# Turning x to token order in the scan: 32x32 blocks on VectorE in place of 128x128 transposes on TensorE

## The reference, cut to what matters

```
xbc = silu(causal_dwconv(xbc, ...));  xs, bm, cm = split(xbc)
x  = xh * dt[..., None]                                      # by token and head
cb = einsum('bclgn,bcsgn->bcgls', cc, bc)                    # B times C, per group and chunk of 128
y_diag = einsum('bcgls,bgrcls,bcsgrp->bclgrp', cb, decay, x) # contracts over tokens s
y = y_diag + y_off + d_skip * xh                             # then gated, normed per group, projected
```

## Time and profile before

| | |
|---|---|
| Median of 3 runs | 1935.86 us |
| The profiled execution's own time | 1935.83 us |
| Its span in the profile | 1934.1 us |
| TensorE matmul busy | 1918.0 us, 99% |
| TensorE weight load busy | 1630.2 us, 84% |
| VectorE busy | 1264.0 us, 65% |
| ScalarE busy | 1083.7 us, 56% |
| GpSimd busy | 34.4 us, 2% |
| HBM read | 358.38 MB, 186 GB/s over the span |
| Transposes of x (L1587) | 64 instructions |

### The profile page before, as it was taken

One profiled execution on the slowest core, in us unless ns is written; L12 is line 12 of the kernel. 1 busy time (PEld: TensorE's weight loads), 2 busy tenths in 40 slices (PEclk: granted clock), 3 DMA queues, 4 the chain that ended last, 5 costly groups with the idle time before them and its releaser, 6 DMA issues.

```text
span 1934.1 us, 28955 instructions
## 1 busy us (share of the span) xinstructions
PE 1918.0 (99%) x10258; PEld 1630.2 (84%) x10258; DVE 1264.0 (65%) x1534; ACT 1083.7 (56%) x1474; POOL 34.4 (2%) x79
## 2 busy tenths in 40 slices
PE   9999999999999999999999999999999999999998
PEld 7888888888887878888888888888888888888886
DVE  6777788777868974544444555766766767745444
ACT  6567766677657764444344444666666666534443
POOL 1000000000000100000000000000000000000000
PEclk9999999999999999999999999999999999999999
DMA  7666666656655437666666565666666666665554
GB/s 244 189 192 177 196 190 192 191 171 196 200 153 138 132 127 213 194 192 194 193 193 195 175 229 191 201 184 186 194 191 190 187 186 191 188 200 193 192 193 141
DMA packets 294839, 361.53 MB, mean 187 GB/s; under 512 B 13104, under 2 KB 217968, under 8 KB 293360
## 3 DMA queue, kind: packets, MB, share of 16 engines
q1 hardware_dynamic: 294768, 360.59, 60.8%
HBM read 358.38 MB, written 2.16 MB: 186 GB/s over the span
## 4 chain that ended last, share of the span: by engine, by line
PE 98%; DVE 1%; ACT 1%; issue 0%; DMA 0%; DVEq 0%; SPq 0%; POOLq 0%; POOL 0%; ACTq 0%
PE ps L1405 35%; PE ps L1407 18%; PE ps L1390 14%; PE ps L1392 13%; PE ps L1391 13%; PE ps L1598 1%; PE ps L1526 1%; PE ps L1539 1%; PE ps L1550 0%; PE ps L1599 0%; PE ps L1587 0%; PE ps L1442 0%; DMA raw<-w_in 0%; ACT hi L449 0%; PE ps L1477 0%
## 5 line engine op out<-in xcount | busy, mean ns | idle before, releaser
L870 DVE TENSOR_TENSOR lo<-raw,hi 128x1024 fp32r<-128x1024 f32 x656 | 799.6, 1224 | 525.5 <-ACT hi L449 518.5
L1405 PE MATMUL ps<-uHL,hi 128*128 128x512 f32 x2944 | 1034.8, 396 | 0.3 <-ACT sgs L666 0.3
L449 ACT ACTIVATE hi<-raw 128x1024 fp32r<-128x1024 f32 x656 | 686.8, 1055 | 514.1 <-PE ps L1392 382.5
L1407 PE MATMUL ps<-uHL,lo 128*128 128x256 f32 x2944 | 823.7, 280 | 0.0
L1405 PEld LDWEIGHTS ps<-uHL,hi 128*128 128x128 f32 x2944 | 551.7, 187 | 130.6 <-issue 5.0
L1407 PEld LDWEIGHTS ps<-uHL,lo 128*128 128x128 f32 x2944 | 555.9, 189 | 0.0
L1392 PE MATMUL ps<-hi,aL 128*128 128x512 f32 x384 | 149.5, 389 | 0.0
L1392 PE MATMUL ps<-hi,hL 128*128 128x512 f32 x352 | 136.9, 389 | 0.0
L1391 PE MATMUL ps<-lo,hH 128*128 128x512 f32 x352 | 136.9, 389 | 0.0
L1390 PE MATMUL ps<-hi,hH 128*128 128x512 f32 x352 | 136.9, 389 | 0.0
L454 ACT ACTIVATE hb<-ps 128x512 f32<-128x512 f32 x92 | 54.7, 595 | 121.5 <-PE ps L1407 121.5
(11 more groups left out here) (195 smaller groups left out, 1654.7 us busy)
## 6 DMA issues: line engine op xcount, KB each, us to landing
raw<-w_in SPq DMA_DIRECT2D x265, 512.0 KB, 4.2
raw<-w_ffn_in SPq DMA_DIRECT2D x176, 512.0 KB, 3.8
raw<-w_ffn_out SPq DMA_DIRECT2D x88, 512.0 KB, 4.4
raw<-w_ssm_out SPq DMA_DIRECT2D x64, 512.0 KB, 4.4
raw<-w_attn_out SPq DMA_DIRECT2D x32, 512.0 KB, 4.3
raw<-w_o SPq DMA_DIRECT2D x32, 512.0 KB, 4.3
rows_b<-cum_rows SPq DMA_DIRECT2D x8, 1024.0 KB, 6.7
x_tok<-x SPq DMA_DIRECT2D x8, 256.0 KB, 6.5
```

Of the source, the lines that this page charges most:

```text
L449: act.activation(hi[:, s % SLOTS, :], raw[:, s % SLOTS, :], ACT.Copy).then_inc(hi_ready, 1)
L870: ve.tensor_tensor(lo[:, s % SLOTS, :], raw[:, s % SLOTS, :], hi[:, s % SLOTS, :].bitcast(F32), ALU.subtract).then_inc(lo_ready, 1)
L1405: pe.matmul(ps[:, pair + c, :], w_hi, uHL[:, kk].rearrange("p a n -> p (a n)"), start=kk == 0, stop=False)
L1407: last = pe.matmul(ps[:, pair + c, 0:SEQ], w_lo, uHL[:, kk, 0, :], start=False, stop=kk == k - 1)
```

## The change

TensorE keeps the two products of B and C and no longer transposes x; `turn_x` becomes `b_dot_c` and the semaphore `x_turned` becomes `bc_done`. VectorE gets a new step `x_turn(k, q)` behind each of the units u = 3, 4, 5, 6. Step q reads the 32 partitions q of x and issues four transposes, one for each 32-partition group j that it writes; each instruction turns eight blocks of 32x32 (4 channel tiles x 2 chunks), 256 numbers for each of its 32 partitions. They write `xd` directly; `ssd_inputs` then multiplies `xd` in place by `dt` instead of reading PSUM, and moves from behind u = 5 to behind u = 6, after the last `x_turn`. Everything else stays in its place.

```diff
+            def x_turn(k, q):
+                ve.wait_ge(sv_ready, k + 1)
+                src = sv[q * B32:(q + 1) * B32, 0:4, :].rearrange("p i (c n) -> p i c n", c=TT)
+                for j in range(P // B32):
+                    dst = xd[j * B32:(j + 1) * B32, :, :].rearrange("p c (i n) -> p i c n", i=4)
+                    ve.transpose(dst[:, :, :, q * B32:(q + 1) * B32], src[:, :, :, j * B32:(j + 1) * B32])
...
             def ssd_inputs(k):
-                ve.wait_ge(x_turned, k + 1)
+                ve.wait_ge(bc_done, k + 1)
                 ve.tensor_tensor(cbm[:].rearrange("p a n -> p (a n)"), ps[:, M, 0:3 * P],
                                  masks[:].rearrange("p a n -> p (a n)"), ALU.mult)
                 for c in range(TT):
-                    ve.tensor_tensor(heads(xd[:, c, :]), heads(ps[:, M + 1 + c, :]), bc(dtt[:, 0, c, ds(k * HG, HG)]),
+                    ve.tensor_tensor(heads(xd[:, c, :]), heads(xd[:, c, :]), bc(dtt[:, 0, c, ds(k * HG, HG)]),
                                      ALU.mult)
...
-            STEPS = dict(inputs=5, low=8, high=9, skip=12, gate=13, sum=17, mean=19)
+            STEPS = dict(inputs=6, low=8, high=9, skip=12, gate=13, sum=17, mean=19)
             def ssd_side(k, u, at=STEPS, older=True):
...
+                if 3 <= u < 7:
+                    x_turn(k, u - 3)
                 if u == at["inputs"]:
                     ve.drain()
                     ssd_inputs(k)
...
-            LAST_STEPS = dict(inputs=5, low=7, high=8, skip=11, gate=12, sum=13, mean=15)
+            LAST_STEPS = dict(inputs=6, low=7, high=8, skip=11, gate=12, sum=13, mean=15)
...
-            def turn_x(k, first=False):
+            def b_dot_c(k, first=False):
                 pe.wait_ge(sv_ready, k + 1)
                 if not first:
                     pe.wait_ge(y_skipped, k)
                 pe.matmul(ps[:, M, 0:2 * P], sv[:, 4, 0:P], sv[:, 5, :], start=True, stop=True)
-                pe.matmul(ps[:, M, 2 * P:3 * P], sv[:, 4, P:SEQ], sv[:, 5, P:SEQ], start=True, stop=True)
-                for c in range(TT):
-                    for i in range(4):
-                        last = pe.transpose(ps[:, M + 1 + c, i * P:(i + 1) * P], sv[:, i, c * P:(c + 1) * P], ident[:])
-                last.then_inc(x_turned, 1)
+                pe.matmul(ps[:, M, 2 * P:3 * P], sv[:, 4, P:SEQ], sv[:, 5, P:SEQ], start=True, stop=True) \
+                    .then_inc(bc_done, 1)
```

More of the change, by code:

```diff
@@ L61 @@
 W5 = 512
+B32 = 32
 U_KV = 0
@@ L238, in build @@
         conv_first, conv_done, sz_ready = sem("conv_first"), sem("conv_done"), sem("sz_ready")
-        decay_ready, x_turned, g_ready = sem("decay_ready"), sem("x_turned"), sem("g_ready")
+        decay_ready, bc_done, g_ready = sem("decay_ready"), sem("bc_done"), sem("g_ready")
         y_done, y_skipped, y_gated, y_squared = sem("y_done"), sem("y_skipped"), sem("y_gated"), sem("y_squared")
@@ L1618, in ssd_after @@
                 if u == at[0]:
-                    turn_x(k, not older)
+                    b_dot_c(k, not older)
                 if u == at[1]:
```

## The result

The kernel after takes 1961.64 us (median of 4 runs, 1959.72 to 1962.45) against 1935.84 us before: a ratio of 1.013, with an interval from 1.0118 to 1.0141. That is 25.8 us more, where the forecast was 12.5 more. The direction and the place are as forecast; the size is twice as large. The shortest run of after is 21.6 us above the longest of before, so the sign is beyond doubt. The profiled execution took 1961.13 us, its span 1959.3 us.

The account below looks back on a forecast made before the run. TensorE was taken to bound the kernel (busy 1918.0 of 1934.1 us). Groups 2 to 7 add 10.2 us, group 1 adds 3.1, the last scan saves 0.8: 12.5 more, 1948.3 us; own range 1944 to 1956, wider 1940 to 1966.

Parts of the forecast that it names:

- TensorE saves 0.8 us a scan: Eight transposes of x leave TensorE before the next unit: 0.79 us a scan, 6.3 us over eight scans.
- 0.34 us apiece: Assumed price of each of VectorE's 128 transposes, start to start; bounds 0.22 and 0.64 us.
- Steps 0 to 2 are hidden: Transposes behind units 3 to 5 need 4.1 us and fit VectorE's 4.5 us of room before `lo` of unit 6.
- the limit, 0.37 us apiece: Transpose price from which steps 0 to 2 would spill over VectorE's room before `lo` of unit 6.
- the sign to look for: If `lo` of unit 6 no longer waits for ScalarE, the transposes are dearer than 0.37 us.
- Step 3 and the inputs: Behind unit 6, not hidden: 3.4 us before `lo` of unit 7; TensorE starts unit 8 1.34 us later.
- The extra wait at the mean: TensorE's mean waits for VectorE's later sum of squares: another 0.2 to 0.25 us a group.
- Group 1: Same steps with less margin at `lo` of unit 8: 3.1 us longer, resume included.
- The last scan: No convolution follows, `lo` of unit 7 comes in time, so this scan keeps its 0.8 us saving.
- The rival of dear transposes: Transposes over 0.45 us apiece on VectorE: 1965 us at 0.5, up to 1983; chance 16%.
- The other signs: Profile after: VectorE busy about 44 us more; TensorE waiting for `lo` 1.5 to 2.5 us a group, none in last scan.
- Loads and later units: Unit 11's later load is ready before VectorE needs it; behind unit 9 TensorE's margin grows again.

Follow-up runs that it names:

- e10: After in e4's order, but VectorE makes one 128x1024 transpose behind unit 1 and GpSimd copies the 16 blocks into place: 1929.81 us, ratio 0.9966.
- e1: After, with TensorE's 64 transposes put back, written to banks that nobody reads: 1959.39 us, ratio 1.0124.
- e3: After, with 24 transposes of the identity on TensorE behind unit 6 of group 1 alone: 1960.78 us, ratio 1.0129.
- e12: After, with the two block loops exchanged, so each step writes one partition group and reads all four: 1960.31 us, ratio 1.013.
- e8: Before, with 22 extra VectorE instructions (transposes, copies, multiplies) in blocks at its end to read their prices: 1943.11 us, one execution.
- e11: Before, with 24 extra VectorE transposes and copies at its end, varying strides and partition groups: 1940.10 us, one execution.
- e4: After, with ScalarE's SiLU behind unit 0, the transposes behind units 1 to 4 and the inputs behind unit 5: 1935.04 us, ratio 0.9994.
- e6: After, with the edits of e4 and e5 together (early SiLU, late convolution): 1939.24 us, ratio 1.0015.
- e5: After, with VectorE's six convolution taps moved from behind unit 7 to behind unit 9: 1959.19 us, ratio 1.0118.
- e2: Before, with only the inputs step (mask and multiply) moved from behind unit 5 to behind unit 6: 1941.63 us, ratio 1.003.

## Why the prediction was right in direction and half in size

**TensorE saves 0.8 us a scan: right, and worth nothing.** It is 0.87 us; e10 shows it where nothing is in its way, and e1 shows that it is swallowed in after.

**0.34 us apiece: the failed step.** The recorded duration, 435 ns, is close to the 426 of the row that I took. What failed is the overlap of 0.09 us, read from two `lo` in sequence, which read and write the same partitions. The new instructions change the group each time. Four take 1.78 to 1.80 us, `lo` behind them starts only at their end (496.71), and the first of them starts 1.26 us after a `lo` instead of 1.14 (497.97 against 496.71): a step costs 1.91 us where 1.36 was written. The Trainium skill (Vector Engine (DVE) Microarchitecture Reference, section 3.8) has a transpose at one element per cycle and lane, from which the prediction's estimate made 0.44 us of duration. The trace agrees with the duration: 0.435, and 1.24 for 1024 numbers in e10. What was wrong is the distance from one start to the next, 0.45 us where the prediction took 0.34.

**Steps 0 to 2 are hidden: wrong in groups 2 to 7 and the last scan, by this term alone.** They need 1.79 + 1.91 + 1.91 = 5.6 us of the 4.5 that the prediction counted, and 1.1 spill over, just what the timeline shows between `hi` and `lo` of unit 6. The prediction had the limit, 0.37 us apiece, and the sign to look for (no wait for ScalarE in front of `lo` of unit 6); both held.

**Step 3 and the inputs: 3.4 us, 4.0 measured.** From `lo` of unit 6 to `lo` of unit 7 there are 6.53 us instead of the 5.93 (2.53 + 3.4) worked out, nearly all of it again the transposes' 0.55. With the 1.1 before it that is 1.7 us in each of six groups on top of the forecast 1.7, so 3.4, as measured. TensorE's waits at units 7 and 8 are at the places named, 4.0 us together where 2.1 were worked out. The extra wait at the mean (0.2 to 0.25) is 0 to 0.3 us in the six groups, 0.12 in the mean. The eight pairs of a unit behind a wait take 0.1 us longer, as the prediction had it, and do so at units 7 and 8 both.

**Group 1, 3.1 against 5.7.** Of the 2.6 us, 1.5 are the clock's: the nine pairs at 1.2 GHz lost 2.7 us and took the place of the wait of 1.2 at unit 8, and at full clock (e3) the group was 1.5 shorter. The prediction had no term for the clock. Of the other 1.1, only 0.4 are the transposes' price. Here steps 0 to 2 were hidden, since `lo` of unit 6 still waited for ScalarE:

```profile
114.01 1.23 DVE L871 TENSOR_TENSOR lo<-raw,hi 128x1024 fp32r<-128x1024 f32 x1 [0.48 <-ACT hi L450]
```

From it to `lo` of unit 7 there are 6.35 us instead of 5.93. Some 0.3 are `hi` of unit 6, which comes that much later counted from the product of B and C, and 0.4 the pairs behind y, 0.354 us apart where group 1 of before has 0.346.

**The last scan, 0.8 less against 0.8 more**: its margin of 0.15 us could not take 1.7.

**The sum.** 12.5 + 10.1 (six groups) + 2.6 (group 1) + 1.6 (last scan) - 1.5 (outside the stretches) = 25.3, against 25.2 of span. No kernel had the change in place at the lower price (e12 was meant to), so the share of the price in these sums is worked out from the timelines and from e8 and e11; that the place decides is shown by e4. The rival of dear transposes, "over 0.45 us apiece (two cycles a number, or no overlap of one with the next)", was the true case by its second condition, though it stood at 16%, since I read the overlap of one kind of instruction as a property of the engine. It gave 1965 for 0.5. The other signs follow the same term: VectorE is busy 55.7 us more and not 44, and the last scan has a wait of 1.56 us where none was expected.

**Loads and later units: right.** TensorE has no wait for `lo` behind unit 8 in any group of after.

## What to carry to other kernels

Spare time of an engine that works in order counts only where it lies: here the same 16 instructions a scan cost 26 us behind units 3 to 6 with the inputs after them, and nothing behind units 1 to 4 with the inputs in their old place. Before moving work to a half-idle engine, list its idle gaps between the source being ready and the next product that the bounding engine waits for, and price a new instruction by the distance of starts, not by a duration less somebody else's overlap. And follow the moved work one wait further: in e6 the gain was lost on a third engine, and in e10 group 1 pays for a fourth.

## What the runs showed of the hardware

- VectorE instructions on 32 partitions overlapped with the next by 0.06 to 0.08 us where both read and wrote the same groups, and not where one of the two changed: transposes of 256 numbers 1.41 against 1.78 us for four, copies 0.89 against 1.18 (e11, e12). `lo` on 128 partitions does not overlap with a step that begins in group 1 to 3 (it ends at 497.94, the transposes begin at 497.97), but the one that begins in group 0 does overlap with the 128-partition instruction before it (494.92 against 495.01). It is so in all eight scans of after and of e12: 0.08 us of overlap ahead of step 0, a gap of 0.03 ahead of steps 1 to 3. So it may be the first partition that must stay; this was read, not tested.
- A VectorE transpose in 32x32 blocks takes 1.24 us for 128x1024 float32, like a subtraction of that size; sixteen of 32x256 take 7.2.
- TensorE's granted clock fell to half behind waits of 2.2 to 3.3 us in some groups and not in others: in after behind the one of 3.29 (group 1) and behind none of the six of 2.13 to 2.49, in e5 in all seven groups (2.17 to 3.06), in e3 in five of six, in e12 in four of seven, in e1 behind the one of 2.21 and behind none of 1.25 to 1.67. What decides between them was not settled.
- The pairs of matmuls start 0.346 or 0.354 us apart for whole units, and change over at a restart of the stream. In group 7 nine units of before run at 0.346, three of after and one of e2, which is some 0.4 us. Over groups 2 to 7 the means are 6.3, 4.5 and 3.3 units, 0.1 to 0.2 us a group. Why is open.
- `lo` (128x1024, two inputs in SBUF) took 1286 ns in the mean, 1422 at most, while GpSimd copied blocks of 32x256 (e10, 32 instructions), and 1224 otherwise (624 instructions). That GpSimd is the cause was not tested by a run of its own.
